# A two-block transformer kernel: six turns of two and five turns of four experts, and a second unit of expert weights loaded ahead

## The reference, cut to what matters

```python
# end of the first block: 32 experts, top 2 of one group of 8
for e in range(N_EXPERTS):
    hid = jax.nn.silu(t @ w_gate[e]) * (t @ w_up[e])      # 1024 -> 512
    y = y + combine[:, e:e + 1] * (hid @ w_down[e])       # 512 -> 1024
...
# start of the second block: the same network on the context and on the tokens
def macaron_ffn(xs, g, shift, scale, gate, w_gate, w_up, w_down):    # 1024 -> 2816 -> 1024
    return xs + 0.5 * gate * swiglu(modulate(xs, g, shift, scale), w_gate, w_up, w_down)
```

## Time and profile before

| | |
|---|---|
| median of 3 runs | 2085.83 us (2085.72 to 2088.5) |
| profiled execution | 2083.22 us, its span 2081.4 us |
| TensorE (PE) busy | 1977.9 us, 95% |
| VectorE (DVE) / ScalarE (ACT) busy | 1251.6 us, 60% / 883.2 us, 42% |
| transfers | 540.59 MB, mean 260 GB/s |

### The profile page before, as it was taken

How to read it: one execution, slowest core, us unless ns; L and a number is a source line. 1 busy time by engine, 2 the same in 40 slices (tenths; PEclk the granted TensorE clock), 3 DMA queues, 4 the chain that set the end, 5 groups by cost and what they waited for, 6 DMA issues and landing times. The chain is left out here.

```text
span 2081.4 us, 32074 instructions
## 1 busy us (share of the span) xinstructions
PE 1977.9 (95%) x13086; PEld 1588.2 (76%) x13086; DVE 1251.6 (60%) x1925; ACT 883.2 (42%) x1341; POOL 48.3 (2%) x56
## 2 busy tenths in 40 slices
PE   7899999999998888889999999989999999999998
PEld 7887798644445665669888888578888888888887
DVE  5977545431113333437777734877778777877776
ACT  4545444311012222227544522665446454545444
POOL 1000000000000000000000100010001000000000
PEclk9999999999999999999999999999999999999999
DMA  9549963799999999997442832054546355666331
GB/s 386 223 176 420 384 249 142 298 382 422 421 421 414 412 420 417 417 421 279 172 187 104 312 146 80 11 217 188 202 159 267 122 233 199 236 269 257 150 124 51
DMA packets 75973, 540.59 MB, mean 260 GB/s; under 512 B 8544, under 2 KB 8736, under 8 KB 12976
## 3 DMA queue, kind: packets, MB, share of 16 engines
q1 hardware_dynamic: 74016, 531.66, 64.0%
q0 software_dynamic: 1520, 6.46, 0.8%
q10 hardware_dynamic: 288, 0.39, 0.1%
HBM read 537.43 MB, written 1.05 MB: 259 GB/s over the span
## 5 line engine op out<-in xcount | busy, mean ns | idle before, releaser
L1330 PE MATMUL lo<-xs,wp 128*128 128x512 f32 (+1 forms) x3392 | 588.9, 335 | 0.3 <-DVE xs L2900 0.2
L1330 PEld LDWEIGHTS lo<-xs,wp 128*128 128x128 f32 x3392 | 511.5, 188 | 74.9 <-issue 1.4
L1001 ACT ACTIVATE wp<-ring 128x1024 fp32r<-128x1024 f32 (+1 forms) x328 | 337.9, 1031 | 247.8 <-PE hi L1330 141.0
L2758 DVE TENSOR_TENSOR wp<-ring,wp 128x1024 fp32r<-128x1024 f32 (+1 forms) x328 | 390.1, 1189 | 7.4 <-ACT wp L1001 6.9
L1330 PE MATMUL hi<-hs,wp 128*128 128x256 f32 (+1 forms) x1842 | 313.9, 331 | 1.3 <-DVE hs L3106 1.1
L1330 PEld LDWEIGHTS hi<-hs,wp 128*128 128x128 f32 x1842 | 273.4, 189 | 38.5 <-DVE hs L3106 1.4
L1330 PE MATMUL lo<-ring,scratch 128*64 128x512 f32 (+1 forms) x1520 | 249.9, 594 | 14.8 <-DMA ring<-in_moe_w_up_dram 8.3
L1330 PEld LDWEIGHTS lo<-ring,scratch 128*64 128x64 f32 (+1 forms) x1520 | 78.4, 123 | 170.9 <-issue 161.5
L2765 DVE TENSOR_TENSOR ring_r<-ring,home 128x1024 fp32r<-128x1024 f32 x52 | 63.0, 1224 | 127.8 <-ACT home L1009 127.8
L1009 ACT ACTIVATE home<-ring 128x1024 fp32r<-128x1024 f32 x52 | 53.9, 1053 | 182.5 <-DMA ring<-in_ffn_up_dram 70.0
L1330 PE MATMUL hi<-xs,home 128*128 128x256 f32 x576 | 105.4, 287 | 9.4 <-DVE ring_r L2765 7.0
(11 more groups left out here) (495 smaller groups left out, 2705.1 us busy)
## 6 DMA issues: line engine op xcount, KB each, us to landing
ring<-in_ffn_up_dram SPq DMA_DIRECT2D x110, 1024.0 KB, 7.5
ring<-in_mod_w_dram SPq DMA_DIRECT2D x72, 1024.0 KB, 10.5
ring<-in_moe_w_up_dram SPq DMA_DIRECT2D x64, 1024.0 KB, 14.3
ring<-in_moe_w_down_dram SPq DMA_DIRECT2D x64, 1024.0 KB, 15.0
ring<-in_moe_w_gate_dram SPq DMA_DIRECT2D x62, 1024.0 KB, 11.7
ring<-in_ffn_w_down_dram SPq DMA_DIRECT2D x32, 1024.0 KB, 9.9
ring<-in_w_in_dram SPq DMA_DIRECT2D x20, 1024.0 KB, 14.1
ring<-in_ffn_w_down_dram SPq DMA_DIRECT2D x20, 768.0 KB, 6.1
```

Of the source, the lines that this page charges most:

```text
L1001: act.activation(wp[:, q % SLOTS, 0, k:k + w.shape[1], :], w, ACT.Copy).then_inc(piece_hi, 2 // len(parts))
L1330: return pe.matmul(dst, lhsT, rhs, start=start, stop=stop, **kw)
L2758: tt(wp[:, q % SLOTS, 1, k:k + w.shape[1], :], w, wp[:, q % SLOTS, 0, k:k + w.shape[1], :].bitcast(F32), ALU.subtract).then_inc(piece_lo, ...
```

## The change

Six turns of two and five of four, instead of eight and four. The added turn of four has twelve expert units and two of the context network, which bring the gate and up pieces of tiles 16 to 19, and no down unit. Behind the turns the pieces of tiles 20 and 21 are done in the early manner, so that the loop over tiles 18 to 21 goes, and down pass 2 begins at once; its first two chunks are cut in two, with the 16 transposes between them. The norm of x is done in another order on ScalarE and VectorE, and `scaled` for FFN 1's input moves into the loop over the output chunks. The first half of the gate weights of turn 3 is loaded ahead too: one expert's into the free half of `ht`, the other's into two free stretches of `scratch`. The context's chunks of `xs` are written in turn 4. The number of bytes loaded is the same.

```diff
-PAIRS, QUADS = 8, 4
+PAIRS, QUADS = 6, 5
-AHEAD = (1, 0, 0)
+AHEAD = ((1, 0, 0), (3, 0, 0))
...
-EARLY_TILES = 18
-EARLY_PIECES = 52
-U_QUADS = U_MOE + 6 * PAIRS - 1
-U_FFN[0] = U_QUADS + 15 * QUADS
-U_FFN[1] = U_FFN[0] + 5
+EARLY_TILES = FTILES
+EARLY_PIECES = 60
+U_QUADS = U_MOE + 6 * PAIRS - len(AHEAD)
+U_FFN[0] = U_QUADS + 15 * QUADS - 1
+U_FFN[1] = U_FFN[0] + 3
...
+        def ahead_row(i, e, k):
+            if i == 1:
+                return ahead.rearrange("p (e k n) -> p e k n", e=2, k=4)[:, e, k]
+            if e == 0:
+                return ht[:, 2 * k:2 * k + 2, 0:T]
+            return part(2560 * (1 + k // 2) + FF * (k % 2), FF)
...
             sp.wait_ge(ex_order, 1)
+            first, second = (expert_of(moe_w_gate, bass.ds(e, 1))[:, 0:4] for e in experts_of(1))
+            for e, rows_in in enumerate((first, second)):
+                sp.dma_start(ahead.rearrange("p (e k n) -> p e k n", e=2, k=4)[:, e], rows_in).then_inc(ahead_loaded, 16)
+            first, second = (expert_of(moe_w_gate, bass.ds(e, 1))[:, 0:4] for e in experts_of(3))
+            sp.dma_start(ht[:, :, 0:T], first.rearrange("p k (b t) -> p (k b) t", t=T)).then_inc(ahead_loaded, 16)
+            for a in range(2):
+                sp.dma_start(part(2560 * (1 + a), 2, FF), second[:, 2 * a:2 * a + 2]).then_inc(ahead_loaded, 16)
...
-                if i == 2:
+                if i == 4:
                     for c in range(KC):
...
-                    if (i, bank, half) == AHEAD:
-                        pe.wait_ge(ahead_loaded, 32)
+                    if (i, bank, half) in AHEAD:
+                        pe.wait_ge(ahead_loaded, 16 * 5)
...
# ScalarE, behind the turns
             round_piece(EARLY_PIECES)
+            for t in range(TT):
+                ...
+                act.activation(part(11264, D), x[:, t, :], ACT.Square, accum_out=ss[:, t:t + 1]).then_inc(norm_sq, 1)
             early_piece(EARLY_PIECES - 2, False)
+            link(act.activation(small[:, 82:83], eps[:], ACT.Sqrt))
+            for t in range(TT):
+                act.activation(std[:, t:t + 1], ss[:, t:t + 1], ACT.Sqrt, ...).then_inc(norm_std, 1)
             act.wait_ge(piece_done, EARLY_PIECES - 1)
             round_piece(EARLY_PIECES + 1)
             early_piece(EARLY_PIECES - 1, False)
...
# TensorE, behind the early pieces
-            for tile in range(EARLY_TILES, FTILES):
-                ...
+            last_down(0, range(5))
+            pe.wait_ge(h_mul, FTILES)
+            pe.wait_ge(xg_ready, TT)
+            ... 16 transposes of x
+            last_down(1, range(5))
+            for d in range(2):
+                last_down(d, range(5, FTILES - 16))
+            pe.wait_ge(rms_sq, 4)
+            ... 8 products with means
+            last_down(2, range(FTILES - 16))
+            pe.wait_ge(fm_copied, 2)
+            for d in range(3, KC):
+                if d == KC - 1:
+                    pe.wait_ge(ev_done, 4 * KC + 4)
+                last_down(d, range(FTILES - 16))
             pe.wait_ge(rms_std, 4)
...
# VectorE, the loop over the output chunks
+            for d in range(KC):
+                if d == 2:
+                    dve.wait_ge(fm_copied, 2)
+                    dve.wait_ge(rms_std, 4)
+                    link(dve.reciprocal(rstd_x, rstd_x))
+                    for c in range(2):
+                        scaled(un[:, c], xT, c, mod_scale[:, 1], rstd_x)
+                early_added(down_q(0, 2, d), d, lo[:, d, 0:T] if d < 3 else hi[:, (d - 2) % 4, 0:T])
                 rest_next(down_q(0, 2, d))
+                if d >= 2:
+                    scaled(un[:, d], xT, d, mod_scale[:, 1], rstd_x)
+                if d >= 4:
+                    norm_lo(1, d - 4, mod[:, 0, 0, 0])
+            for c in range(KC - 4, KC):
+                norm_lo(1, c, mod[:, 0, 0, 0])
```

More of the change, by code:

```diff
@@ L279, in up_unit @@
             if f == 0:
[L280 removed]
+                return U_FFN[0] if c == NCHUNK - 1 else U_QUADS + 15 * (c // 2) + 5 * (c % 2)
             return U_FFN[f] + c + 2 * ((c > 4) + (c > 8))
@@ L285, in down_units @@
             if f == 0:
-                return tuple(U_FFN[0] + 3 + j if p == 2 else U_QUADS + 15 * (2 * p + j) + 10 for j in range(2))
+                return tuple(U_FFN[0] + 1 + j if p == 2 else U_QUADS + 15 * (2 * p + j) + 10 for j in range(2))
             return tuple(U_FFN[f] + (5, 11, 15)[p] + j for j in range(2))
@@ L1057, in _ @@
                 expert_silu(i)
-                for j in range(4, 10):
-                    early_piece(q + j, j < 10)
-                expert_turned(i)
[L1061 to L1064, removed]
+                more = 10 if i < EX_TURNS - 1 else 6
+                for j in range(4, more):
+                    early_piece(q + j, True)
+                if i == EX_TURNS - 1:
+                    early_piece(q + 6, False)
+                expert_turned(i)
+                early_piece(q + more + (i == EX_TURNS - 1), False)
+                if i < EX_TURNS - 1:
+                    early_piece(q + 11, False)
+                early_round(q + more + 2)
+                early_round(q + more + 3)
                 expert_out(i)
@@ L1705, in expert_up @@
                         n = u_expert(i, bank, half, e // 2)
-                        ins = places(i, e, n, bank, hg[:, 4 * half + k, :], expert_cols(n, e % 2)[:, k, :], half + k == 0, half == 1 and k == 3)
+                        ins = places(i, e, n, bank, hg[:, 4 * half + k, :], ahead_row(i, e, k) if n is None else expert_cols(n, e % 2)[:, k, :], half + k == 0, half == 1 and k == 3)
                         if k == 3 and e % 2 and n is not None:
@@ L1869, in _ @@
                     scatter_rows(i - 1, 1)
-                for j in range(4, 8):
+                more = 8 if i < EX_TURNS - 1 else 6
+                for j in range(4, more):
                     early_piece(q + j)
@@ L2018, in ffn, with last_down @@
                 downs(f, 2, stats)
[L2020 to L2023, removed]
+            def last_down(d, chunks):
+                q = down_q(0, 2, d)
+                if chunks[0] == 0:
                     pe.wait_ge(piece_lo, 2 * q + 2)
[L2025 to L2038, removed]
@@ L2039, in _ @@
-            pe.wait_ge(rms_std, 4)
[L2040 to L2047, removed]
-                    late_step(q, hi[:, d % 4, 0:T], k, FTILES - 16, hs)
-                if d >= 2:
-                    squared(0, d - 2)
+                for k in chunks:
+                    if d < 2:
+                        pe.wait_ge(h_lo, 17 + k)
+                    late_step(q, lo[:, d, 0:T] if d < 3 else hi[:, (d - 2) % 4, 0:T], k, FTILES - 16, hs)
@@ L2051, in _ @@
+            for c in range(KC):
+                ins = mm(lo[:, 3, 0:T], means[:, 1, :], un[:, c, :], c == 0, c == KC - 1)
+            ins.then_inc(rms_ms, 1)
+            last_down(2, range(FTILES - 16))
[4 more added lines that the diff above has]
+                last_down(d, range(FTILES - 16))
+            pe.wait_ge(rms_std, 4)
             for d in (KC - 2, KC - 1):
```

120 lines of the change are left out of this document (56 added, 64 removed).

## The result

The changed kernel takes 2091.06 us (median of 20 runs, 2086.87 to 2443.41); the kernel before takes 2088.47 us beside it (20 runs, 2084.27 to 2095.45). The ratio is 1.0018, with an interval of 1.0009 to 1.0026: slower by 0.2%, where 2074.7 us and a gain of 0.5% were forecast. The 2443.41 is one slow execution, which the ratio leaves out; the next highest is 2096.72. The profiled execution has a span of 2087.3 us.

What follows compares the result with a forecast made beforehand. Transfers were taken to bound the turns of four, TensorE the rest of the context network. 5.0 + 0 + 2.3 + 1.0 - 19.4 = -11.1 us, applied to the 2085.8 us median, gave 2074.7 us; 80% range 2069 to 2081.

Steps and rivals of the forecast that it cites:

- the last turn: Last turn of four: 48 us of TensorE work within 70 us of transfers, so no cost except a clock term.
- The sign named for being wrong: At the unit where the expert turns end: the prediction is wrong if its start moves by more than 12 us.
- the first turn of four: Start of the turns of four: DMA fills the ring and idles until a slot frees, +2.3 us, bounds 0 and 6.
- One unit more on the ring: Before the border unit: the last expert unit's ring index goes from 106 to 107, one transfer more, +5.0 us.
- the second unit ahead refilling gaps: From 405 to 480 us: the added early load fits into DMA gaps of 6.2 us, cost 0, bounds 0 and 5.
- Rival 1: The second unit ahead is paid for, its gaps not refilled: gain only 6.1 us, 2079.7 us; chance 0.15.
- The tail: From the border unit's first matmul to FFN 1: 61.9 to 42.5 us, -19.4, bounds -23.3 and -15.
- rival 2: Behind the border VectorE does not bind, and no low clock: 4.0 us more gain, 2070.7 us; chance 0.10.
- The low clock at the border: First piece behind the border: TensorE may start it at the 1.2 GHz level, +1.0 us, bounds 0 and 3.
- Rival 3: The ht half loaded ahead, in 1 KB pieces, crawls and holds the queue before turn 1: 2092 us; chance 0.04.
- Rival 4: Ring stalls of 2.9 us instead of 0.7 in each of five turns of four: no change, 2086 us; chance 0.04.

Runs made afterwards that it cites:

- after, again: The changed kernel run once more, unchanged, against the kernel before: ratio 1.0016 (1.0002 to 1.0031).
- last turn mended: Changed kernel with all gate and up pieces of the last turn of four ahead of the experts' up products: 2078.47 us, ratio 0.9964 to the kernel before.
- both mended: Changed kernel, last turn's pieces all ahead of its up products, and experts' gate units ahead of the context's first unit in the first turn of four: 2075.93 us, 0.9957.
- one unit ahead: Changed kernel with one unit of expert weights loaded ahead instead of two, the second back in the ring: ratio 1.0015 to the kernel before.
- last turn mended, one unit ahead: Changed kernel with all last-turn pieces ahead of the up products and only one unit loaded ahead: 2077.9 us, ratio 0.9956 to the kernel before.
- first turn mended only: Changed kernel with the experts' gate units and products ahead of the context's first unit and pieces in the first turn of four: ratio 1.0008 to the kernel before.

## Why the prediction was wrong

**The step that failed** is in the part on the last turn: "It has eight pieces and no down unit of its own: TensorE has 48 us of work in 70 us of transfers. Its last down half waits about 6 us for its unit", and the sum has no term for this turn but the clock's. (The 48 us don't follow from its own figures either, which make 51; nothing hangs on that.) It took the last turn's transfers as running by themselves. The change moves two pieces behind a wait of TensorE, and the text followed them on TensorE only, where they are indeed free (it idles 7.34 us behind them). What they hold is a slot, and through it SP's queue and every unit behind: 10.6 to 11.3 us of idle transfers in the two executions, 13.3 us of border when the pieces are moved back (1.4 of them at the first turn of four, which lost 6.8 us there against a mean of 8.2). The sign named for being wrong, a border that moves by more than 12 us, was there: 24.7.

**The term that was mis-sized** is the first turn of four: 2.3 us, bounds 0 and 6, measured 6.7 and 9.7. It took 631.81 as the landing of the first context unit, but that is when ScalarE began on it, and the row shows no wait for a DMA. The issue is at 604.48 and lands 22.0 us later in this row of the kernel before:

```profile
ring<-in_ffn_up_dram SPq DMA_DIRECT2D x2, 1024.0 KB, 22.0
```

That is 626.5, and 13 units earlier 561.8. The ring is then full at 586.7, not 592.0; the window of 580 to 590 with its 2.1 us lost puts it at 587.9. On the other side TensorE frees its first slot at 595.9 instead of 592.3: its scatter (576.78) takes 3.56 us at a low clock, and the pieces start at 582.72 instead of 580.5 (the forecast's own rows, 7.9 less the 1.15 of the slower scatter, give 6.8 us of gap and not its 7.1). Together 9.2 us, near the 9.7 of the windows.

The other steps, by the account of transfers (two units more up to the border, 10.0 us in all, against idle time gained and lost, in us; the border before is the mean of two, the 386 GB/s of the first column those of its first execution):

| kernel | 405 to 480 | first turn | last turn | sum with 10.0 | border moved |
|---|---|---|---|---|---|
| after | -4.8 | +9.7 | +11.3 | 26.2 | 26.4 |
| after, again | -4.8 | +6.7 | +10.6 | 22.5 | 22.9 |
| last turn mended | -4.8 | +6.8 | 0 | 12.0 | 11.4 |
| both mended | -5.5 | +7.6 | 0 | 12.1 | 12.8 |
| one unit ahead | 0 | +5.3 | +11.4 | 26.7 | 26.7 |
| last turn mended, one unit ahead | -1.4 | +3.7 | 0 | 12.3 | 13.8 |
| first turn mended only | -4.6 | +5.7 | +11.9 | 23.0 | 23.1 |

Idle time outside these windows, as from 640 to 660 (0.9 and 2.4 us in the kernel before, 0 to 2.0 in those of the table), is left out, and the scatter of the border before (528.1 and 530.6) is in every row.

- One unit more on the ring, +5.0, and the second unit ahead refilling gaps: right, 4.8 of its 5.0 us came back at 405 to 480 (3.4 against the second execution of the kernel before). Rival 1 is refuted in its own terms. What neither had seen is that most of the lead is lost again at the first turn of four, in the changed kernel only.
- The tail, -19.4: right. Measured -17.6 to FFN 1 from the first matmul in the profiled execution, and 61.94 to 42.85 = -19.1 once the first piece no longer starts cold. The transposes wait 1.78 us (2.6 forecast), the reciprocal starts at S + 27.6 (27.1). VectorE binds in front of FFN 1 as worked out: it works without a gap from 988.67 on and ends the third weight piece at 1006.54, just before FFN 1, while TensorE idles 2.29 us. So rival 2 is out. (Its -4.0 should have been -4.7, 3.7 us of waiting and 1.0 of clock.)
- The low clock at the border, +1.0: it came as described. The first pair of matmuls takes 0.80 us against 0.51 in the earlier trace rows; 1.5 us of stretch compared with the mended kernel.
- Rival 3, pieces of 1 KB: refuted. The ht half and the two behind it are issued at 406.3 and 406.9, the next ring unit at 411.69, and the DMA moves 393 and 398 GB/s from 400 to 410 and 410 to 420, where the rival needed less than 77. That its 2092 us lie beside the measured 2091 is chance. The Trainium skill, "DMA: Bandwidth & Descriptors", section "Specifications", has line rate from 512 B up; the trace agrees.
- Rival 4 had the right sign of the mistake (ring stalls eat the gain) and the wrong place: not a little in five turns, but in the first and in the last.

What the change set out to do is worth 0.4% with its last turn in the old order (0.9964), and about as much without the second unit ahead (0.9956).

## What to carry to other kernels

When a step is moved, look at what it *releases*, not only at what it waits for: with slots refilled in order, a piece that is free on its own engine can hold the load that this very engine waits for next. Reckon the lead of the transfers from issue plus time to landing, never from the consumer's first instruction unless its row shows a wait for the DMA. And a load put ahead is worth its time only if TensorE waits for a unit before the ring is next full: it was worth 0.24% with eight turns of two, and nothing measurable with six. Idle transfers summed over windows gave the shift of the border within 1.5 us in the seven executions of the table.

## What the hardware showed besides

A stage far behind the change, the same 1146 matmuls at a granted clock of 1.00, takes 190.7 us in one execution and 193.7 in another, and either kernel has shown both lengths (the kernel before 193.70 and 190.71, the changed kernel 190.56 and 193.70). The first row is of the kernel before in its second run, the second of the changed kernel in its second run (windows, columns as in rows 1):

```profile
1400.54:1591.25 190.71, 190.21 (x1146) 166.16 (x1143) 145.69 (x222) 101.98 (x156) 5.90 (x6) 1.00 0.54 205
```

```profile
1399.53:1593.23 193.70, 193.43 (x1146) 166.47 (x1142) 145.78 (x222) 101.96 (x156) 5.90 (x6) 1.00 0.53 201
```

TensorE is busy in all of either; a wait does not explain it, and the columns shown don't. Nothing here tells the cause. The 3 us are more than lies between the medians of the two kernels (2.6 us), so that a single span can't decide such a change. Neither can a single position: FFN 1 differs by 3.9 and 3.7 us between the two executions of either kernel. The timed ratios can, and a trace can where the shift is large, as the 24.7 us of the border. From FFN 1 to the end the profiled executions of all kernels here take 1079.1 to 1086.7 us, so that the 6.2 us at FFN 1 and the 2.6 of the medians are no contradiction, and no closer account of the difference can be given.
